# Splitting each 512-column TensorE product of a three-product float32r matmul into two of 256 columns

## The reference

```
for l in range(2):
    mod  = silu(cond) @ w_ada[l] + b_ada[l]           # -> shift, scale, gate
    h    = rmsnorm(x, norm_pre[l]) * (1 + scale) + shift
    proj = h @ w_in[l]                                # 384 x 2048 times 2048 x 5120
    if l % 2 == 0: o = [silu(g_a) * attention(q, k, v), silu(g_b) * dft_mix(u_b)]
    else:          o = [silu(g_c) * pooling(u_c),       silu(g_d) * gating(u_d, v_d)]
    x    = x + gate * rmsnorm(o @ w_out[l], norm_post[l])   # 384 x 2048 times 2048 x 2048
```

## Time and profile before

| | |
|---|---|
| Median of 2 runs | 1113.76 us (1113.72 to 1113.79) |
| Span of the profiled execution, first to last instruction | 1113.0 us |
| TensorE matmul records (PE) | 1091.5 us busy, 98% of the span, 5356 |
| TensorE weight loads (PEld) | 879.1 us busy, 79%, 5356 |
| VectorE (DVE) | 705.0 us, 63% |
| ScalarE (ACT) | 427.3 us, 38% |
| DMA | 242.28 MB, 218 GB/s over the span |
| Mean granted TensorE clock | 0.995 |

### The profile page before, as it was taken

The page is one execution under the profiler, slowest core; times in us unless marked ns, Lnnn a source line. Parts: engine busy times, 40 slices in busy tenths (PEclk is TensorE's granted clock), DMA queues, the critical chain, the costliest instruction groups (busy, mean ns, idle before and its releaser), DMA issues.

```text
span 1113.0 us, 13620 instructions
## 1 busy us (share of the span) xinstructions
PE 1091.5 (98%) x5356; PEld 879.1 (79%) x5356; DVE 705.0 (63%) x1029; ACT 427.3 (38%) x693; POOL 33.4 (3%) x66
## 2 busy tenths in 40 slices
PE   6999999999999999999999999999999999999997
PEld 5576687887878878888888788888888888888885
DVE  4555575767677787699966645487665766343335
ACT  4333334433636432243346852223423223243332
POOL 1000010000000000000010000000000000000000
PEclk8999999999999999999999999999999999999999
DMA  9998866454545567567884235345644554433423
GB/s 381 407 394 337 339 242 250 166 228 162 216 193 214 211 272 303 228 236 295 315 325 153 83 145 188 135 170 190 211 172 184 210 206 159 183 133 132 155 72 114
DMA packets 39327, 242.28 MB, mean 218 GB/s; under 512 B 4784, under 2 KB 4896, under 8 KB 13408
## 3 DMA queue, kind: packets, MB, share of 16 engines
q1 hardware_dynamic: 29232, 190.85, 44.8%
q0 software_dynamic: 7344, 46.29, 11.5%
q10 hardware_dynamic: 2688, 4.26, 1.4%
HBM read 237.67 MB, written 3.72 MB: 217 GB/s over the span
## 4 chain that ended last, share of the span: by engine, by line
PE 95%; DVE 2%; ACT 1%; DMA 1%; issue 1%; DVEq 0%; ACTq 0%; SPq 0%
PE bank L966 27%; PE bank L968 26%; PE bank L967 26%; PE bank L1030 3%; PE bank L1112 2%; PE bank L1051 1%; PE bank L1176 1%; PE bank L1128 1%; PE bank L1091 1%; PE bank L1135 1%; DMA x_t<-in_x_turned 1%; PE bank L917 1%; PE bank L915 1%; PE bank L916 1%; PE bank L1101 0%
## 5 line engine op out<-in xcount | busy, mean ns | idle before, releaser
L966 PE MATMUL bank<-w_hi,h_op 128*128 128x512 f32 x1114 | 450.0, 404 | 2.6 <-DVE h_op L1761 2.2
L968 PE MATMUL bank<-w_hi,h_op 128*128 128x512 f32 x1114 | 435.4, 391 | 0.0
L967 PE MATMUL bank<-w_lo,h_op 128*128 128x512 f32 x1114 | 434.5, 390 | 0.0
L1509 DVE TENSOR_TENSOR w_lo<-raw,w_hi 128x1024 fp32r<-128x1024 f32 x200 | 244.3, 1222 | 191.3 <-ACT w_hi L1221 190.9
L1221 ACT ACTIVATE w_hi<-raw 128x1024 fp32r<-128x1024 f32 x200 | 210.0, 1056 | 227.3 <-PE bank L968 211.8
L966 PEld LDWEIGHTS bank<-w_hi,h_op 128*128 128x128 f32 x1114 | 209.4, 188 | 58.0 <-issue 15.6
L968 PEld LDWEIGHTS bank<-w_hi,h_op 128*128 128x128 f32 x1114 | 209.1, 188 | 45.2
L967 PEld LDWEIGHTS bank<-w_lo,h_op 128*128 128x128 f32 x1114 | 209.6, 188 | 39.5
L966 PE MATMUL bank<-w_hi,o_low 128*128 128x512 f32 x192 | 75.8, 395 | 0.0
L968 PE MATMUL bank<-w_hi,o_low 128*128 128x512 f32 x192 | 74.9, 390 | 0.0
L967 PE MATMUL bank<-w_lo,o_low 128*128 128x512 f32 x192 | 74.8, 390 | 0.0
(11 more groups left out here) (227 smaller groups left out, 929.8 us busy)
## 6 DMA issues: line engine op xcount, KB each, us to landing
raw<-in_w_in SPq DMA_DIRECT2D x68, 1024.0 KB, 5.3
dot_raw<-in_ada_tiles POOLq DMA_DIRECT2D x32, 1024.0 KB, 5.1
raw<-in_w_out SPq DMA_DIRECT2D x32, 1024.0 KB, 4.9
raw_first<-in_ada_first SPq DMA_DIRECT2D x21, 1024.0 KB, 11.1
raw<-in_ada_groups SPq DMA_DIRECT2D x16, 1024.0 KB, 6.7
raw<-in_ada_halves SPq DMA_DIRECT2D x16, 1024.0 KB, 4.7
open_raw<-in_w_in SPq DMA_DIRECT2D x24, 512.0 KB, 11.5
dot_raw<-in_ada_first SPq DMA_DIRECT2D x11, 1024.0 KB, 10.1
```

The source lines that it names most:

```text
L966: pe.matmul(out, operand(layer, kind, 0, k, t), hi, start=k == begin, stop=False)
L967: pe.matmul(out, operand(layer, kind, 0, k, t), lo, start=False, stop=False)
L968: last = pe.matmul(out, operand(layer, kind, 1, k, t), hi, start=False, stop=k == end)
L1509: dve.tensor_tensor(w_lo[:, half % WRING, :, :].rearrange("p k n -> p (k n)"), src, hi, ALU.subtract)\
```

## The change

The three matmuls of a triple become six. A new helper `products` cuts the 512 columns into two halves of `HALF_CW` = 256 and issues, for the left half of the bank, high times `w_hi`, high times `w_lo` and low times `w_hi`, and then the same three for the right half. The `start` flag stands only on the first matmul of the left half. `skip_group_check` is a flag for the builder. All three functions call the helper. Semaphore increments stay on the last matmul of the triple, waits stay where they were, and no other engine's program changes.

```
+HALF_CW = CW // 2
...
+            def products(out, high, low, hi, lo, start, stop):
+
+                for a in range(0, CW, HALF_CW):
+                    cols = slice(a, a + HALF_CW)
+                    pe.matmul(out[:, cols], high, hi[:, cols], start=start and a == 0, stop=False, skip_group_check=True)
+                    pe.matmul(out[:, cols], high, lo[:, cols], start=False, stop=False, skip_group_check=True)
+                    last = pe.matmul(out[:, cols], low, hi[:, cols], start=False, stop=stop, skip_group_check=True)
+                return last
...
-                    pe.matmul(out, operand(layer, kind, 0, k, t), hi, start=k == begin, stop=False)
-                    pe.matmul(out, operand(layer, kind, 0, k, t), lo, start=False, stop=False)
-                    last = pe.matmul(out, operand(layer, kind, 1, k, t), hi, start=False,
-                                     stop=k == end)
+                    last = products(out, operand(layer, kind, 0, k, t), operand(layer, kind, 1, k, t), hi, lo,
+                                    k == begin, k == end)
```

More of the change, by code:

```diff
@@ L914, in tile_steps @@
                     lo = w_lo[:, half % WRING, k % 2, :]
-                    pe.matmul(out, operand(layer, kind, 0, k, t), hi, start=False, stop=False)
-                    pe.matmul(out, operand(layer, kind, 0, k, t), lo, start=False, stop=False)
-                    last = pe.matmul(out, operand(layer, kind, 1, k, t), hi, start=False, stop=k == KT - 1)
+                    last = products(out, operand(layer, kind, 0, k, t), operand(layer, kind, 1, k, t), hi, lo,
+                                    False, k == KT - 1)
                     if t == FINAL and k % 2:
@@ L980, in late_tile @@
                     lo = w_lo[:, half % WRING, k, :]
-                    pe.matmul(out, operand(1, "uc", 0, k, FINAL), hi, start=k == 0, stop=False)
-                    pe.matmul(out, operand(1, "uc", 0, k, FINAL), lo, start=False, stop=False)
-                    last = pe.matmul(out, operand(1, "uc", 1, k, FINAL), hi, start=False, stop=False)
+                    last = products(out, operand(1, "uc", 0, k, FINAL), operand(1, "uc", 1, k, FINAL), hi, lo,
+                                    k == 0, False)
                 last.then_inc(mm_done, 1)
```

## The result

The changed kernel takes 1157.26 us (1157.21 to 1157.32) against 1113.76 us: a ratio of 1.039, with a 95% interval of 1.037 to 1.041. That is 43.5 us more, where 10.9 us were forecast. The span of the profiled execution is 1155.4 us against 1113.0 us.

What follows compares the result with a forecast made beforehand. TensorE's stream was taken to bound the kernel; 4032 products x 2.7 ns = +10.9 us on the 1113.0 us span gave 1123.9 us, about 1125 us (+1.0%) on the runs' median, with a range of 1101 to 1172 us.

Steps and rivals of the forecast that it cites:

- What bounds the kernel: Whole kernel: TensorE's stream sets the time, with PE records over 98% of the span and 95% of the chain.
- the counts: Three product lines: 4032 products of 512 columns at 226.7 ns, 914 us or 82% of the span, become 8064 halves.
- the price of 1 ns: TensorE's stream: a nanosecond more per product is a nanosecond more of time, counted over 4032 products.
- The weight load: One load per product: needs 109 to 112 ns, so it costs nothing behind a half product of 114.7 ns.
- Rival 4: Weight loads: each occupies its path for its whole 188 ns record; +602 us, 1716 us; chance 0.01.
- The 13.3 ns: Each 512-column product's time beyond its columns: 2.7 ns per instruction, 10.6 ns with the columns; pair 229.4 ns, +2.7 ns.
- It does not come from the weight load that runs beside it: Product at 607.31 us: no load beside it, yet its record is as long as the others, 0.39 us.
- It is not constant: After side products: float32r products come at 230 ns, then settle at 226.7 ns, unlike a fixed set-up per instruction.
- float32 has hardly any of it: Float32 products: they ask for half as many columns a nanosecond and carry only 2.7 ns beyond their columns.
- Rival 1: Each of 8064 halves: the excess is per instruction, 120.0 ns a half; +53.6 us, 1167 us; chance 0.38.
- Rival 2: Halves: excess vanishes, only the load is left; -13 us, 1100 us, or -35 us, 1079 us; chance 0.07.
- rival 3: Load and matmul pairs: TensorE cannot be handed them that fast for long; at 125 ns +94 us, 1208 us; chance 0.06.

Runs made afterwards that it cites:

- e1: Changed kernel with each 512-column product issued as four of 128 columns instead of two of 256; 1986.95 us (one run).
- e5: Changed kernel, but products that do not start a bank's sum load only 32 of 128 activation columns and write only 32 rows; 1132.42 us.
- e6: Kernel before (512-column products) with the weight loads cut to 32 activation columns where a product does not start a bank's sum; 1125.26 us.
- e10: Changed kernel with weight loads of 64 activation columns, and 64 rows written, where a product does not start a bank's sum; 1117.96 us.
- e13: Changed kernel (256 columns) with w_hi and all placed after it in SBUF moved up by 64 bytes; 1140.7 us.
- e15: Kernel before (512 columns) with w_hi and all placed after it in SBUF moved up by 64 bytes; 1120.4 us.
- e11: Changed kernel (256 columns) with w_hi and all placed after it in SBUF moved up by 32 bytes; 1134.3 us.
- e12: Changed kernel with every SBUF tensor moved up by 32 bytes, activations and weights alike; 1157.9 us.
- e4: Changed kernel with only the third product (low times w_hi) cut in halves, the first two left at 512 columns; 1129.95 us, 1.015.

## Why the prediction was wrong

**What bounds the kernel, the counts, the price of 1 ns.** Right. 8064 products, PE 96% of the chain, no new waits, other engines untouched. One nanosecond per product was worth somewhat less than the 4.03 us by count: 43.5 us / 13.3 ns = 3.3 us, since the uneven stretches do not follow the settled distance. The prediction had not looked at what they would do.

**The weight load.** Right: 109 to 112 ns, and 111.7 ns when it is the bound (e1); behind a half product it is not the bound. Rival 4 is excluded by that: PEld is busy for 95% of the span with records of 192 ns, and is not the bound. By the Trainium skill's "Perfetto Trace Analysis", section "Identifying the Most-Contended Engine", that share is one of two measures of how far TensorE is used; as a measure of what room is left the traces do not bear it out, since it was 79% before, and yet twice as many loads fit, one every 120.0 ns.

**The 13.3 ns.** This step failed: "So I take 2.7 ns as the charge per instruction (the float32 value, the nearest row) and 10.6 ns as belonging to the columns. A half is then [...] 114.7 ns". Measured: 120.0 ns. A charge of about 2.7 ns per instruction is what bfloat16 has (2.5 ns at either width). The rest, 10.6 ns, was taken for proportional to the columns. At a 32-byte shift the whole excess is proportional (20.0 and 10.0 ns); at the kernel's own place a half carries as much as the whole, 13.3 ns, so the pair costs 13.3 ns more and not 2.7. Nothing in the trace before said which of the two holds at which place, and I took the one case for a law.

**The three readings behind it.** "It does not come from the weight load that runs beside it" was read from one row with a length of 0.39 us. To the nanosecond that product is 1 ns shorter than its neighbours (388 and 389 ns), so for the whole product the reading stands; the corresponding half product is 4 ns shorter, which the row of a whole product could not say. A narrower load changes the pace as well (e5, e6, e10), in either direction. The fault lies in what was made of the reading: an excess that is not the load's need not be the columns'. "It is not constant" was right, and it was the useful observation: the same product came at 226.7, 230 and, between halves, 233 ns, and so has no fixed charge of 13.3 ns. But it is no charge per column either. That float32 has hardly any of it was right as well.

**The rivals.** Rival 1 gave 120.0 ns and 1167 us; its distance is met to the tenth, its total is 10 us too high because of the uneven stretches. The signs that the prediction gave for it, a record of 283 ns and a distance of 120 ns, are both there. Yet its mechanism is not what runs, and that its number came out is the luck of this one place: a charge per instruction would be the same at every shift, and it is +13.3, 0, +6.9 and +5.1 ns. With a chance of 0.38 it stood beside the forecast's 0.48, so the doubt was stated. It also lay inside the stated range, as the measured time does (1101 to 1172 us). But a forecast of +1.0% for a change of +3.9% is a miss of the size by a factor of four, and the likeliest case was named wrongly. Rival 2 is excluded by the 120.0 ns themselves, rival 3 by e1.

**What stays open.** Why a certain distance between the two operands gives a certain excess, and why the same stream can settle at one pace or at another (e5, e10, e13, e15). The settled steps at one place are all alike (120 ns), at others they go through a cycle of three or more values (e11: 121, 113, 116, 117 ns). That the moving and the stationary operand's reads meet in SBUF would fit that e11 moves the pace and e12 does not, but the meeting itself is in no record, and the products with no load beside them keep more than half of their excess, so it cannot be the whole account. A shift also moved `w_lo` and the buffers behind it; `h_op`, `o_low` and the loaded `raw` stayed. It was not tried to move `w_lo` against `w_hi`, and no distance beyond 128 bytes was.

## What to carry to other kernels

Before a dense TensorE stream is cut finer, take a product's distance apart into columns, a charge per instruction and a rest, and find out what the rest hangs on; here it was worth 1 or 44 us for the same edit. A float32r stream is sensitive to where its operands lie relative to each other: two versions of this kernel whose buffers were moved differed by up to 2% for that alone. A pace read in one stretch need not hold in the next, so read several. Where the accuracy allows it, bfloat16 parts gave 216 ns in place of 227 ns per 512 columns, and 4.1% of this kernel; whether they too feel a shift was not run.

## What the runs showed of the hardware that was not expected

- A float32r product of 512 columns takes 13.3 to 20.0 ns beyond its columns at 2.4 GHz, by the relative place of its operands in SBUF; 32 bytes make a difference of 6.7 ns a product and 19.5 us in the kernel (1113.8 and 1133.3 us). The Trainium skill's "TensorE: Matmul & The Clock Gate", section "Step-by-step: what each phase is for", says that loading the next weights does not take read bandwidth from the running matmul. For bfloat16 nothing here speaks against it. For float32r these runs do in part: the last half product, with no load beside it, is 4 ns shorter (279 and 283 ns). But more than half of the excess is there without a load, and in e15 the last product is no shorter without one (397 ns, neighbours 391 ns).
- One float32r stream can settle at two paces: 113.3 and 117.8 ns for 256 columns with loads of 32 columns (e5), 228.9 and 233.3 ns for 512 columns at a shift of 64 bytes (e15). Among halves, whole products come at 233 ns in place of 226.7 ns at an unchanged place (e4).
- A smaller load can be worse: 231.7 ns with 32 columns against 226.7 ns with 128, for 512 columns.
- Weight loads of 128 float32r columns can follow each other at 111.7 ns over a whole kernel, with PEld records of 192 ns.
